# Stick-breaking attention: steps taken in pairs, with four turn banks and one score bank

## What is computed

```python
def stick_breaking_attention(q, k, v):
    """A[t,s] = beta[t,s] * prod_{s<j<t} (1-beta[t,j]), s<t only."""
    ...
        z = jnp.einsum('bthd,bshd->bhts', q[:, t0:kend], k[:, :kend]).astype(jnp.float32) * scale
        mask = s_idx < t_idx
        log_beta = jax.nn.log_sigmoid(z)
        log_rem = jnp.where(mask, jax.nn.log_sigmoid(-z), 0.0)
        after = lax.cumsum(log_rem, axis=3, reverse=True) - log_rem
        w = jnp.where(mask, jnp.exp(log_beta + after), 0.0)
        outs.append(jnp.einsum('bhts,bshd->bthd', w.astype(v.dtype), v[:, :kend]))

def mixer_stick_breaking(h, w_in, w_out):
    proj = jnp.einsum('bsd,de->bse', h, w_in)
    q, k, v, g = jnp.split(proj, 4, axis=-1)
    ...
    return jnp.einsum('bse,ed->bsd', o * jax.nn.silu(g), w_out)
```

## Time and profile before

| | |
|---|---|
| time, median of three runs | 1680.17 us (1679.1 to 1680.67) |
| profiled execution: its time | 1680.25 us |
| profiled execution: its span | 1678.5 us |
| mean granted TensorE clock | 0.998 |
| first scores | about 212 us |
| last weighing | 1496 us |

### The profile page before, as it was taken

The page is one execution under the profiler, slowest core; times in us unless marked ns, Lnnn a source line. Parts: engine busy times, 40 slices in busy tenths (PEclk is TensorE's granted clock), DMA queues, the critical chain, the costliest instruction groups (busy, mean ns, idle before and its releaser), DMA issues.

```text
span 1678.5 us, 23276 instructions
## 1 busy us (share of the span) xinstructions
PE 1649.8 (98%) x8600; PEld 1377.5 (82%) x8600; DVE 1338.3 (80%) x1879; ACT 906.1 (54%) x1773; POOL 235.0 (14%) x212
## 2 busy tenths in 40 slices
PE   7999999999999999999999999999999999999998
PEld 6888878888888888888888888888888888778786
DVE  4436478889898889888988988898888888956765
ACT  6625355565565555656555655665555556661222
POOL 0020012110211011102110211011101110008400
PEclk9999999999999999999999999999999999999999
DMA  9858634342524243334333342425243434398732
GB/s 293 273 159 266 199 119 138 101 148 67 152 75 132 78 143 98 104 101 120 111 97 109 105 133 68 138 82 145 64 136 95 127 92 146 120 357 282 238 138 100
DMA packets 162785, 237.09 MB, mean 141 GB/s; under 512 B 49776, under 2 KB 90736, under 8 KB 162672
## 3 DMA queue, kind: packets, MB, share of 16 engines
q1 hardware_dynamic: 93184, 160.02, 30.4%
q10 hardware_dynamic: 69488, 75.58, 15.1%
HBM read 155.78 MB, written 79.76 MB: 140 GB/s over the span
## 4 chain that ended last, share of the span: by engine, by line
PE 85%; DVE 4%; DMA 4%; ACT 2%; POOL 2%; issue 1%; SPq 1%; ACTq 0%; DVEq 0%
PE proj_ps L714 28%; PE turn_ps L741 13%; PE proj_ps L674 11%; PE z_ps L731 7%; PE z_ps L732 7%; PE o_ps L755 7%; PE o_ps L756 7%; PE turn_ps L785 3%; PE z_ps L785 2%; POOL w_raw L650 1%; DMA gate<-gate_cols 1%; PE proj_ps L785 1%; DMA wo_raw<-in_w_out 1%; DVE u L1125 1%; DMA w_raw<-in_w_qkg 1%
## 5 line engine op out<-in xcount | busy, mean ns | idle before, releaser
L903 ACT ACTIVATE u<-z_ps 128x512 f32<-128x512 f32 (+3 forms) x640 | 341.8, 534 | 409.1 <-PE z_ps L732 405.2
L1125 DVE TENSOR_TENSOR_SCAN u<-u,u 128x512 f32<-128x512 f32 x384 | 491.8, 1281 | 0.0
L1130 DVE TENSOR_TENSOR r_turned_lo<-turn_ps,r_turned_hi 128x512 fp32r<-128x512 f32 (+3 forms) x640 | 377.5, 590 | 34.7 <-ACT r_turned_hi L909 33.0
L909 ACT ACTIVATE r_turned_hi<-turn_ps 128x512 fp32r<-128x512 f32 (+3 forms) x640 | 340.2, 532 | 60.2 <-issue 43.0
L650 POOL TENSOR_SCALAR w_raw<-w_raw,a_norm_col 128x128 f32<-128x128 f32 x192 | 176.7, 938 | 1207.4 <-DMA w_raw<-in_w_qkg 1207.4
L741 PE MATMUL turn_ps<-ident,u 128*128 128x128 f32 x2176 | 342.9, 273 | 0.0
L714 PE MATMUL proj_ps<-hT_hi,w_hi 128*128 128x512 f32 x768 | 320.2, 417 | 0.0
L714 PE MATMUL proj_ps<-hT_lo,w_hi 128*128 128x512 f32 x768 | 320.0, 417 | 0.0
L714 PE MATMUL proj_ps<-hT_hi,w_lo 128*128 128x512 f32 x768 | 319.8, 416 | 0.0
L741 PEld LDWEIGHTS turn_ps<-ident,u 128*128 128x128 f32 x2176 | 267.8, 140 | 58.9 <-DVE u L1125 0.2
L755 PE MATMUL o_ps<-r_turned_hi,dv_head 128*128 128x512 f32 (+3 forms) x640 | 231.5, 362 | 8.0 <-DVE r_turned_lo L1130 3.8
(11 more groups left out here) (106 smaller groups left out, 1645.6 us busy)
## 6 DMA issues: line engine op xcount, KB each, us to landing
x_T<-in_xT SPq DMA_DIRECT2D x32, 512.0 KB, 5.9
qk_hi_cols<-made_hi ACTq DMA_DIRECT2D x64, 256.0 KB, 2.8
qk_lo_cols<-made_lo ACTq DMA_DIRECT2D x64, 256.0 KB, 3.2
w_raw<-in_w_qkg SPq DMA_DIRECT2D x24, 512.0 KB, 3.4
x_rows<-in_x SPq DMA_DIRECT2D x16, 512.0 KB, 4.5
v_rows<-v_stage ACTq DMA_DIRECT2D x32, 256.0 KB
v_here<-v_rows SPq DMA_DIRECT2D x64, 128.0 KB, 2.9
v_next<-v_rows SPq DMA_DIRECT2D x64, 128.0 KB, 3.1
```

The source lines that it names most:

```text
L903: nc.scalar.activation(u_t[(m // CB) % RU][STEPS[m][3]][:, 0:w], z_ps[m % RZ][:, 0:w], ACT.Sigmoid, scale=-Z_SCALE).then_inc(s_u, 1)
L909: nc.scalar.activation(rt_hi[m % RT][:, 0:w], t_ps[m % RT][:, 0:w], ACT.Copy).then_inc(s_hi, 1)
L1125: nc.vector.tensor_tensor_scan(u, u, other, start, ALU.mult, op).then_inc(s_r, 1)
L1130: nc.vector.tensor_tensor(rt_lo[m % RT][:, 0:w], t_ps[m % RT][:, 0:w], as_f32(rt_hi[m % RT][:, 0:w]), ALU.subtract).then_inc(s_lo, 1)
```

## The change

Iterations are taken two at a time (`PAIR = 2`), n and n+1. TensorE now runs: `turn(n+2)`, `turn(n+3)`, three products of the projection (`FILL_FIRST`), `scores(n+10)`, the rest of the pair's products (three or four), `weigh(n)`, `weigh(n+1)`, `scores(n+11)`. ScalarE: `empty`, `hi(n+2)`, `hi(n+3)`, `stick(n+10)`, `store_o`, for both steps `store_made`, `weight_hi` and `dv_hi`, then `made_high`, `stick(n+11)`, and then the gate's pieces and `out_weight_high`. VectorE's loop is not changed, nor are SyncE's and GpSimd's, except that they begin one step earlier and that the step in which some groups end is one earlier.

Scores run ten steps ahead instead of nine. There are four turn banks and one score bank, four pairs of tiles for the turned parts, and one `o_stage` instead of two. `FILL_NUM` is 675 instead of 677.

```diff
-LEAD_SCORES = 9
+LEAD_SCORES = 10
-RU, RZ, RT, RO, RP = 3, 2, 3, 2, 2
+RU, RZ, RT, RO, RP = 3, 1, 4, 1, 2
+PAIR = 2
+FILL_FIRST = 3
-FILL_NUM, FILL_DEN = 677, 200
+FILL_NUM, FILL_DEN = 675, 200
...
-                for n in range(-LEAD_SCORES, NS):
+                for n in range(-LEAD_SCORES, NS, PAIR):
+                    for m in range(n, n + PAIR):
+                        if inside(m + LEAD_TURN):
...
+                            turn(m + LEAD_TURN)
+                    begin, end = filled(n - 1), filled(n + PAIR - 1)
+                    middle = min(begin + FILL_FIRST, end)
+                    project(begin, middle)
                     if inside(n + LEAD_SCORES):
                         scores(n + LEAD_SCORES)
-                    if inside(n + LEAD_TURN):
...
-                        turn(n + LEAD_TURN)
-                    project(filled(n - 1), filled(n))
-                    put_out(out_filled(n - 1), out_filled(n))
-                    if inside(n):
-                        weigh(n)
+                    project(middle, end)
+                    put_out(out_filled(n - 1), out_filled(n + PAIR - 1))
+                    for m in range(n, n + PAIR):
+                        if inside(m):
+                            weigh(m)
+                    if inside(n + 1 + LEAD_SCORES):
+                        scores(n + 1 + LEAD_SCORES)
...
-                for n in range(-LEAD_SCORES, LAST_PIECE_STEP + 1):
+                for n in range(-LEAD_SCORES, LAST_PIECE_STEP + 1, PAIR):
+                    pair = range(n, n + PAIR)
                     ended = chunk_end(n - 1) if inside(n - 1) else None
                     if ended is not None:
                         empty(ended)
+                    for m in pair:
+                        if inside(m + LEAD_TURN):
+                            hi(m + LEAD_TURN)
                     if inside(n + LEAD_SCORES):
                         stick(n + LEAD_SCORES)
                     if ended is not None:
                         store_o(ended)
-                    if inside(n + LEAD_TURN):
-                        hi(n + LEAD_TURN)
-                    for g in GROUPS_DONE.get(n - 3, []):
-                        store_made(g)
-                    for g in GROUPS_DONE.get(n, []):
-                        made_high(g)
...
+                    for m in pair:
+                        for g in GROUPS_DONE.get(m - 3, []):
+                            store_made(g)
+                        if m in HI_W:
+                            weight_hi(HI_W[m])
+                        if m in PAIR_HI:
+                            dv_hi(*PAIR_HI[m])
+                    for m in pair:
+                        for g in GROUPS_DONE.get(m, []):
+                            made_high(g)
+                    if inside(n + 1 + LEAD_SCORES):
+                        stick(n + 1 + LEAD_SCORES)
```

More of the change, by code:

```diff
@@ L40 @@
 AT_U = BASE + 32 * KB
-AT_RT = BASE + 56 * KB
+AT_RT = [(BASE + a * KB, BASE + b * KB) for a, b in ((56, 58), (60, 62), (64, 66), (82, 92))]
 AT_DV = BASE + 68 * KB
@@ L290, in all_stages @@
         u_t = [[place(nc, f"u{n}_{r}", [P, CH], F32, AT_U + 2 * KB * (CB * n + r)) for r in range(CB)] for n in range(RU)]
-        rt_hi = [place(nc, f"r_turned_hi{n}", [P, CH], F32R, AT_RT + 4 * KB * n) for n in range(RT)]
-        rt_lo = [place(nc, f"r_turned_lo{n}", [P, CH], F32R, AT_RT + 4 * KB * n + 2 * KB) for n in range(RT)]
+        rt_hi = [place(nc, f"r_turned_hi{n}", [P, CH], F32R, at[0]) for n, at in enumerate(AT_RT)]
+        rt_lo = [place(nc, f"r_turned_lo{n}", [P, CH], F32R, at[1]) for n, at in enumerate(AT_RT)]
         o_st = [place(nc, f"o_stage{n}", [P, CH], F32, AT_OST + 2 * KB * n) for n in range(RO)]
@@ L320, in all_stages @@
         p_ps = [pb(f"proj_ps{n}") for n in range(RP)]
-        row_ps = z_ps + t_ps[:2]
-        y_ps = [p_ps, z_ps, t_ps[:2], [t_ps[2], o_ps]]
+        row_ps = t_ps
+        y_ps = [p_ps, z_ps + t_ps[3:], t_ps[:2], [t_ps[2], o_ps]]
         s_ident = sem("ident_ready")
@@ L595, in _ @@
                         sp.wait_ge(s_gst, stores_through(GROUP_OF["g", LAST_G - 1, NC - 1]))
-                        for par in range(2):
-                            sp.wait_ge(s_oout[par], 32 * 2 * LAST_G * NC // 2)
+                        for par in range(RO):
+                            sp.wait_ge(s_oout[par], 32 * 2 * LAST_G * NC // RO)
                         load_group(0, slice(0, LAST_G), s_in[0])
@@ L794, in _ @@
                 last.then_inc(s_vturned, 1)
-                for n in range(-LEAD_SCORES, NS):
+                for n in range(-LEAD_SCORES, NS, PAIR):
+                    for m in range(n, n + PAIR):
+                        if inside(m + LEAD_TURN):
+                            if m + LEAD_TURN == 2:
+                                pe.wait_ge(s_vT, 1)
+                            turn(m + LEAD_TURN)
+                    begin, end = filled(n - 1), filled(n + PAIR - 1)
+                    middle = min(begin + FILL_FIRST, end)
+                    project(begin, middle)
                     if inside(n + LEAD_SCORES):
                         scores(n + LEAD_SCORES)
-                    if inside(n + LEAD_TURN):
-                        if n + LEAD_TURN == RT - 1:
-                            pe.wait_ge(s_vT, 1)
-                        turn(n + LEAD_TURN)
-                    project(filled(n - 1), filled(n))
-                    put_out(out_filled(n - 1), out_filled(n))
-                    if inside(n):
-                        weigh(n)
+                    project(middle, end)
[5 more added lines that the diff above has]
+                        scores(n + 1 + LEAD_SCORES)
                 pe.wait_ge(s_u, NS)
@@ L1023, in _ @@
                         store_o(ended)
-                    if inside(n + LEAD_TURN):
-                        hi(n + LEAD_TURN)
-                    for g in GROUPS_DONE.get(n - 3, []):
-                        store_made(g)
-                    for g in GROUPS_DONE.get(n, []):
-                        made_high(g)
[L1030 to L1039, removed]
+                    for m in pair:
[10 more added lines that the diff above has]
+                        stick(n + 1 + LEAD_SCORES)
+                    for m in pair:
+                        if m in SUM_AT:
+                            piece_start(SUM_AT[m])
+                        if m in GATE_AT:
+                            piece_high(GATE_AT[m])
+                        if m - 4 in WO_AT:
+                            out_weight_high(WO_AT[m - 4])
                 for t in range(1, TG):
```

## The result

The changed kernel takes **1693.9 us** (median; 1691.8 to 1695.6), the kernel before 1679.6 in the same series; the ratio is 1.0087, with a 95% interval of 1.0075 to 1.010: slower by 14 us. The forecast was 1696, slower.

A forecast was written before the change was run, and what follows sets the result against it. TensorE, busy 98% of the span, was taken as the bound. Turns 0, VectorE's stop +19.1, score bank +3.2, vanished waits -5.6 gave +16.7; less 0.9 for coinciding stops, 1680.2 + 15.8 = 1696 us, range 1679 to 1708.

The forecast's parts named there:

- VectorE's stop for `made_hi`: VectorE waits at made_low for ScalarE's made_high, so low parts and weighings come late: +19.1 us.
- late even-step groups: Groups ending in a pair's first step: 23 make VectorE late, by 0.8 us in the mean, 18.5 us.
- Step 589: Weighing in the pair after the group ending in step 586: TensorE was to stand 0.6 us.
- odd-step groups: Groups ending in a pair's second step: nearly nothing lost, two late by 0.6 us together.
- What goes away: Late weighings from ScalarE held up by GpSimd vanish: -5.6 us, bounds 2 to 5.6; waits for the group's DMA stay.
- 19.1 less 5.6 and 0.9: VectorE's stop, less late weighings that vanish, less 0.9 us for stops that fall on one place.
- One score bank: Scores wait for the previous sigmoid where ScalarE's w_hi waits for GpSimd: +3.2 us, between 0 and 6.
- the sign of being wrong: TensorE's waits before scores, for the sigmoid, expected at some 3 us; reaching 10 us would show the prediction wrong.
- Turns in pairs: TensorE's turns cost 0.11 us a block, nothing for entering or leaving: term 0, bounds 3 us either way.
- The sum: Whole kernel: terms give +16.7 us, less 0.9 for coinciding stops; 1680.2 + 15.8 = 1696 us.
- Rival B: Faster: the fourth turn bank gives more reserve than pairing takes, 1674.6 or 1671 us; chance 0.12.
- Rival C: The score bank decides: late sigmoids stop TensorE in half the pairs, some 1712 to 1728 us; chance 0.06.

The follow-up runs named there:

- experiment 1: The changed kernel with VectorE's made_low of groups ending in an even step moved one step later: 1674.8 us, ratio 0.9968.
- experiment 3: The changed kernel with ScalarE's made_high of groups ending in an even step moved ahead of the pair's first sigmoid: 1676.1 us, ratio 0.998.
- experiment 4: The changed kernel with ScalarE's and VectorE's halves of the weight tiles three steps later: 1690.6 us, ratio 1.0065.
- experiment 6: The changed kernel with the edits of experiment 1 and experiment 4 together: 1667.5 us, ratio 0.9928.
- kernel 7: The kernel before, old order and banks, with weight-tile halves three steps later and finished groups' stores and low halves one step later: 1674.0 us, ratio 0.9967.
- experiment 5: The kernel of experiment 1 with a pair's two turns, and ScalarE's copies of them, put apart again: 1685.3 us, ratio 1.0031.

## Why the prediction was right

**The mechanism and its size.** VectorE's stop for `made_hi`, set by the parity of the step in which a group ends: shown by experiments 1 and 3, each of which takes away 16 to 17 us of waits by moving one end of it. I had 23 late even-step groups with 18.5 us; the trace has 22 with 18.1. Step 589 was worked out at 0.6 and lost 0.67. For the odd-step groups I had 0.6, and found 3.1 in five places. Four of the five are still there in experiment 1, and all five are gone in experiments 4 and 6, so it was the weight tiles that made them late, which my sum kept apart from the groups.

**What goes away.** Taken at 5.6, and about right. At the places where before had late weighings with GpSimd at their root after has none but 0.6 near step 390, though the same cause shows up at others, as just said; the waits that begin with the group's DMA are 2.2 in place of 3.6. Together, the waits before weighings grew by 11.5 where the terms (19.1 less 5.6 and 0.9) have 12.6.

**One score bank.** Term 3.2. Three waits behind a late `w_hi`, as priced, came to 4.3 (1.7, 1.1 and 1.5, before scores 170, 290 and 568), and 0.5 before score 92 was the long store issue of experiment 4. But four more stand in the first pairs, 3.8 us where one of 1.1 stood before. The largest of them, 2.2 before score 1, has the first sigmoid behind two stores and a load of ScalarE's table, of 1.28. The sum went only through the steady part. These rows of after show it:

```profile
214.11 0.33 ACTq L894 DMA_DIRECT2D qk_hi_cols<-made_hi  x1
214.47 0.46 ACTq L895 DMA_DIRECT2D qk_lo_cols<-made_lo  x1
214.97 0.28 ACT L1022 ACTIVATE v_first_T<-turn_ps 128x128 f32<-128x128 f32 x1 [1.61 <-DVE made_lo L1127]
215.26 1.28 ACT L912 ACT_TABLE_LOAD   x1
```

Before carried the same load and stores; its second score bank let score 1 start without them. In all +7.1 before scores, 3.9 more than the term. The prediction expected some 3 us there and took 10 as the sign of being wrong; 8.4 is nearer to the second.

**Turns in pairs: the term that was wrong.** It stood at 0, with a bound of 3 us. The reading of the block itself holds (0.11 for each block; a run of eight takes 0.88 against 0.89 for two runs of four), but the reading stopped at the second product behind it. The cost lies in products 2 to 7, up to 9 ns each, and in the one before the block: 6.3 us less in after, 7.8 between kernels 7 and 6, 9.3 with the turns put apart. A remainder smaller than the 10 ns resolution of the rows, times several products, times 320 blocks, doesn't show in one pair of rows; the median distance of products by their place would have shown it in the trace of before.

**The sum.** 1696 against 1693.9 looks closer than its parts, and that is luck: -6.3 for the turns and -1.1 before weighings were balanced by +3.9 before scores and +1.9 before the first product of the output, which waits for `wo_hi`. The term for what goes away also did not see that this last wait only changes its place, since 2.1 of the late weighings of before are the same late `wo_hi`. Rival B's hope was there in substance, since the pair order is faster than before by 5 us once the stop is gone, but the stop itself was there, against what B hoped. Rival C fails: one bank costs where ScalarE is late, at 13 products of 9 scores, not in half the pairs.

## What to carry to other kernels

When steps are merged, look for the instruction of another engine that stops in the middle of its program, and go through both parities of where it falls; here the whole loss of 14 us, and a gain of 5 us behind it, hung on the place of one such instruction. When banks are taken from one rotation for another, read for each rotation how much time lies between the last reader and the next writer, at the start of the loop too. When an instruction is moved out of the way of one engine, look at what it then stands behind on the next. And before a cost is set to nothing for lack of a difference between two rows, average over all its occurrences and over the instructions behind it.

## What the runs showed of the hardware

On TensorE at a granted clock of 1.00, 512 wide fp32r products follow each other in 226.7 ns (mean in the stages without turns). Behind a block of fp32 transposes the median is 227 to 236 in places 2 to 7, and 232 to 233 right before such a block; in after it is 227 from the eighth place on, while in the kernel with the turns apart the ninth place, where the next block is near, still has 231. The 6.3, 7.8 and 9.3 us, over 320 blocks, make 20 to 29 ns that each block of transposes, short or long, costs outside itself. The records show it, and experiment 5 shows that it follows the blocks; what in the engine does it stays open. From the start of a block to the second product behind it, less one product, the medians are 0.113 us for one 128 by 128 transpose, 0.443 for four and 0.878 for eight, so 0.109 for each further one.

The granted clock fell to 0.50 for 3.4 or 6.8 us in the middle of ten of the eleven profiled executions, and 512 wide products then started 0.427 us apart. Each time it fell during or within 1.4 us after a stop in which two starts on TensorE lay 2.1 to 3.9 us apart (at 1562.0 in before, 1514.1 in after). Not every such stop did it: in experiment 3 one of 2.9 us did not.
